# Two-block transformer on one core: retention heads turned inside the output product, a router with its weights stationary, the last expert by halves

## The reference

```python
logits = x @ w_router                     # 1024 x 8
top_val, top_idx = top_k(logits, 2); wts = softmax(top_val)
for e in range(8):                        # w_gate, w_up: 1024 x 3584, w_down: 3584 x 1024
    out = out + gates[..., e:e+1] * ((silu(x @ w_gate[e]) * (x @ w_up[e])) @ w_down[e])
x = layer_norm(ALPHA * x + out)
```

## Time and profile before

| | |
|---|---|
| runs | 1864.13 us median of 3 (1861.27 to 1864.32) |
| profiled execution, its own time | 1865.61 us |
| span of its trace, first to last instruction | 1863.8 us |
| TensorE busy | 1744.8 us (94%) |
| VectorE busy | 1416.8 us (76%) |
| ScalarE busy | 1028.3 us (55%) |
| GpSimd busy | 47.8 us (3%) |
| moved by DMA | 531.20 MB |
| mean granted TensorE clock | 0.970 of full |

### The profile page before, as it was taken

One profiled execution on the slowest core, in us unless ns is written; L12 is line 12 of the kernel. 1 busy time (PEld: TensorE's weight loads), 2 busy tenths in 40 slices (PEclk: granted clock), 3 DMA queues, 4 the chain that ended last, 5 costly groups with the idle time before them and its releaser, 6 DMA issues.

```text
span 1863.8 us, 23299 instructions
## 1 busy us (share of the span) xinstructions
PE 1744.8 (94%) x9360; PEld 1487.5 (80%) x9360; DVE 1416.8 (76%) x1241; ACT 1028.3 (55%) x828; POOL 47.8 (3%) x42
## 2 busy tenths in 40 slices
PE   2999899999889999997999999999999999999995
PEld 2988678878679997996888878878878888788784
DVE  7786856475965554775888988879879899798895
ACT  2343244553233333334777767768677777777672
POOL 0000002000000000001000000000000000000200
PEclk9999899999989999997999999999999999999997
DMA  9688354514727573554999999999999999999992
GB/s 366 213 334 298 129 207 152 181 57 154 230 99 270 182 270 136 204 204 147 363 365 382 386 352 389 376 377 375 367 367 364 372 376 377 373 387 370 366 386 96
DMA packets 217771, 531.20 MB, mean 285 GB/s; under 512 B 7600, under 2 KB 14016, under 8 KB 217408
## 3 DMA queue, kind: packets, MB, share of 16 engines
q1 hardware_dynamic: 210624, 514.52, 75.6%
q10 hardware_dynamic: 5712, 10.41, 1.5%
q0 software_dynamic: 1328, 4.73, 0.7%
HBM read 521.94 MB, written 16.09 MB: 289 GB/s over the span
## 4 chain that ended last, share of the span: by engine, by line
PE 70%; DVE 4%; DMA 2%; ACT 2%; issue 2%; POOL 0%; SPq 0%; POOLq 0%; DVEq 0%; ACTq 0%
PE psum L785 22%; PE psum L787 21%; PE psum L786 21%; DMA ring<-in_moe_w_gate 2%; DVE units L1607 2%; PE psum L1151 1%; PE psum L1052 1%; ACT units L1489 1%; PE psum L1005 0%; DVE R L1954 0%; PE psum L1089 0%; PE psum L1116 0%; PE psum L1124 0%; POOL root_out L1556 0%; PE psum L1023 0%
## 5 line engine op out<-in xcount | busy, mean ns | idle before, releaser
L1607 DVE TENSOR_TENSOR units<-ring,units 128x2048 fp32r<-128x2048 f32 x451 | 1010.9, 2278 | 258.9 <-ACT units L1258 151.8
L1489 ACT CAST units<-ring 128x2048 fp32r<-128x2048 f32 x332 | 624.4, 1912 | 239.5 <-PE psum L787 70.9
L785 PE MATMUL psum<-units,xr 128*128 128x512 f32 x1120 | 445.5, 398 | 14.2 <-DVE units L1607 7.1
L787 PE MATMUL psum<-units,xr 128*128 128x512 f32 x1120 | 439.5, 392 | 0.0
L786 PE MATMUL psum<-units,xr 128*128 128x512 f32 x1120 | 438.8, 392 | 0.0
L1258 ACT CAST units<-ring 128x2048 fp32r<-128x2048 f32 (+1 forms) x119 | 218.5, 1880 | 233.8 <-PE psum L787 186.4
L785 PE MATMUL psum<-units,H 128*128 128x512 f32 x696 | 274.5, 394 | 2.1 <-DVE H L1607 2.1
L787 PE MATMUL psum<-units,H 128*128 128x512 f32 x696 | 272.5, 391 | 0.0
L786 PE MATMUL psum<-units,H 128*128 128x512 f32 x696 | 272.4, 391 | 0.0
L785 PEld LDWEIGHTS psum<-units,xr 128*128 128x128 f32 x1120 | 212.2, 189 | 61.9 <-issue 7.8
L785 PE MATMUL psum<-xr,units 128*128 128x256 f32 x864 | 248.4, 287 | 7.3 <-DVE xr L1607 3.8
(11 more groups left out here) (260 smaller groups left out, 1007.2 us busy)
## 6 DMA issues: line engine op xcount, KB each, us to landing
ring<-in_moe_w_gate SPq DMA_DIRECT2D x56, 2048.0 KB, 9.7
ring<-in_moe_w_up SPq DMA_DIRECT2D x56, 2048.0 KB, 9.7
ring<-in_moe_w_down SPq DMA_DIRECT2D x56, 2048.0 KB, 9.6
ring<-in_mod_w SPq DMA_DIRECT2D x12, 2048.0 KB, 10.0
ring<-in_ret_w_in SPq DMA_DIRECT2D x11, 2048.0 KB, 9.6
ring<-in_fox_w_in SPq DMA_DIRECT2D x8, 2048.0 KB, 8.8
ring<-in_sc_w_in SPq DMA_DIRECT2D x6, 2048.0 KB, 8.2
ring<-in_ffn_w_gate SPq DMA_DIRECT2D x5, 2048.0 KB, 9.9
```

What stands on the lines that cost most here:

```text
L785: mm(dst, left[0], right[0], start=first, stop=False)
L787: return mm(dst, left[1], right[0], start=False, stop=last)
L1489: nc.scalar.copy(*expert_unit_parts(q, j, half, 0)).then_inc(unit_high, 1)
L1607: return v.tensor_tensor(dst, src, high.bitcast(F32), ALU.subtract)
```

## The change

Three places, in the order of the program.

**Retention.** `ret_read(2)` moves ahead of `token_chunk("ret_g", 3)`. The head's rows are first made without the root, `(o - mean) * silu(g)` in one VectorE pass, and ScalarE multiplies by the root (`ret_scale`). Head 0 is turned before `ret_read(3)`, heads 1 and 2 after it, and head 3 inside the output product after its first four blocks. The two `mod_w` loads of the second layer's gate, their sums and `mod_sum(1, GATE)` move from the output product and the fox queries to the fox values and gates.

**Router.** The router's 8 columns are stationary, the tokens move; the result (8 x 256) is copied and turned back by two transposes. Of VectorE's work after the choice only the slots stay ahead of the gather; the gates, the places, `e_acc` and the overflow flag come behind it. The first gather is split in two halves. VectorE reads the flag `over` before the experts.

**Last expert.** In the last four blocks of `down` the left half of the columns is finished first, put back and added while the right half is computed. The last layer norm stands at the end of the last expert, ahead of the branch, with both roots asked for at once; after the branch VectorE asks for two roots that nothing uses, since GpSimd's list of roots is fixed and now has those of the second sweep too.

```diff
-               CHUNK_AT["ret_out", 1]: [(1, GATE, 0)], CHUNK_AT["ret_out", 2]: [(1, GATE, 1)]}
+               CHUNK_AT["fox_g", 0]: [(1, GATE, 0)], CHUNK_AT["fox_g", 1]: [(1, GATE, 1)]}
...
-    g += [("ret_o", i, "D") for i in range(4)]
+    g += [("ret_o", i, "D") for i in range(6)]
     g += [("ret_g", i, "A") for i in range(6, 8)]
-    g += [("ret_o", i, "D") for i in range(4, 8)]
-    g += [("ret_uT", i, "S") for i in range(8)]
+    g += [("ret_uT", i, "S") for i in range(2)] + [("ret_o", i, "D") for i in range(6, 8)]
+    g += [("ret_uT", i, "S") for i in range(2, 8)]
...
             ret_read(0)
             ret_read(1)
+            ret_read(2)
             token_chunk("ret_g", 3)
...
+            ret_turn(0)
+            ret_read(3)
+            for h in range(1, RH - 1):
+                ret_turn(h)
+            out_product("ret_out", ruT, RV // P, lambda g: wait_emptied("ret_uT", g), lambda: ret_turn(RH - 1))
...
+            for k in range(KB):
+                if k % 2 == 0:
+                    wait_emptied("x5T", k // 2)
+                last = mm(b[0:NE, 0:T], w_router[:, k, :], x5T[:, k, :], start=(k == 0), stop=(k == KB - 1))
...
             for tt in range(NT):
-                for k in range(KB):
-                    last = mm(b[:, tt * NE:(tt + 1) * NE], x5T[:, k, tt * P:(tt + 1) * P], w_router[:, k, :],
-                              start=(k == 0), stop=(k == KB - 1))
+                last = nc.tensor.transpose(b[:, tt * NE:(tt + 1) * NE], scoresT[:, tt * P:(tt + 1) * P], ident[0:NE, 0:NE])
...
+                    halves = by_matmul(e, more, number) and k >= EB - ROWS
+                    for c in range(1 if halves else 2):
+                        last = down(k, c, w)
...
+                for k, w in late.items():
+                    if k == EB - ROWS // 2:
+                        pe.wait_ge(down_low, matmul_returns(e, number) + 1)
+                        scatter(0)
+                    last = down(k, 1, w)
...
+            def ret_scale(h):
+                act.wait_ge(root_ready, ROOTS.index(f"ret{h}") + 1)
+                wait_emptied("ret_o", 2 * h + 1)
+                for tt in range(NT):
+                    u = rg[:, tt, h * RHV:(h + 1) * RHV]
+                    nc.scalar.activation(u, u, ACT.Identity, scale=root_out[:, ROOTS.index(f"ret{h}") % 2, tt:tt + 1]
+                                         ).then_inc(ret_u_ready, 1)
...
-            high_in("ret_uT", ruT[0], 8)
+            high_in("ret_uT", ruT[0], 6)
+            highs_until(CHUNK_AT["ret_g", 3] + 2)
+            ret_scale(RH - 1)
+            high_in("ret_uT", ruT[0], 8, 6)
...
+            for h in range(RH - 1):
+                ret_head(h)
+            low_in("ret_uT", ruT, 2)
+            ret_head(RH - 1)
+            low_in("ret_uT", ruT, 6, 2)
+            lows_until(CHUNK_AT["ret_out", 1])
+            low_in("ret_uT", ruT, 8, 6)
+            lows_until(CHUNK_AT["ret_out", 3] + 1)
...
             select(0, 0)
+            low_half(CHUNK_AT["sc_out", 1] + 2, 1)
+            dve.wait_ge(first_high, 1)
+            low(e_x[0][1][:, 0:4, :], ...).then_inc(first_low, 1)
+            dve.wait_ge(gather_high, 1)
+            low(e_x[0][1][:, 4:8, :], ...).then_inc(gather_emptied, 1)
+            gates()
             places()
-            gathered(0, 0)
-            sweeps(dve, expert, start_second)
-            layer_norm("out", 4, e_acc, out_g, out_b)
+            for q in range(NT):
+                first_sums(q)
+            dve.wait_ge(up_emptied, 2)
+            overflow()
+            dve.wait_ge(sums_begun, NT)
+            sweeps(dve, expert, start_second, dve.value_load(over[0:1, 0:1], min_val=0, max_val=1))
+            for tt in range(NT):
+                ask_root(f"out1_{tt}", meanvar[:, tt, 1:2], 1.0, LN_EPS)
```

The end of the last expert on VectorE (`add_half(c)` waits for `scatter(c)` and adds 512 columns of each tile to `e_acc`):

```diff
+                    for c in range(2):
+                        dve.wait_ge(down_high, 2 * n + c + 1)
+                        low(e_y[1][:, cs], psum[:, c, :], e_y[0][:, cs]).then_inc(down_low if c == 0 else down_emptied, 1)
+                        if c == 0:
+                            add_half(0)
...
+                                    last = v.bn_stats(stats[:, tt, 0, :], e_acc[:, tt, 0:512])
...
+                add_half(1)
...
+                for tt in range(NT):
+                    ask_root(f"out{number}_{tt}", meanvar[:, tt, 1:2], 1.0, LN_EPS)
+                for tt in range(NT):
+                    v.scalar_tensor_tensor(x[:, tt, :], e_acc[:, tt, :], meanvar[:, tt, 0:1], out_g, ALU.subtract, ALU.mult)
+                for tt in range(NT):
+                    r = root(f"out{number}_{tt}")
+                    v.scalar_tensor_tensor(x[:, tt, :], x[:, tt, :], r[:, 0:1], out_b, ALU.mult, ALU.add)
```

More of the change, by code:

```diff
@@ L669, in sweeps @@
                 sweep(1)
+                if after is not None:
+                    after()
         block = ctx.enter_context(nc.Block())
@@ L853, in out_product @@
                 for k in range(blocks - tail):
+                    if k == ROWS and between is not None:
+                        between()
                     if k % 2 == 0:
@@ L948, in _, with ret_turn @@
             ret_read(1)
+            ret_read(2)
             token_chunk("ret_g", 3)
-            ret_read(2)
-            ret_read(3)
-            for h in range(RH):
+            def ret_turn(h):
                 pe.wait_ge(ret_u_ready, 2 * (h + 1))
@@ L1133, in wide_product @@
                 for half in range(2):
+                    if first and half == 1:
+                        pe.wait_ge(gather_emptied, 1)
                     w = expert_unit(e, q, j, half, lambda a: as_cols(a, 4))
@@ L1167, in expert, with down, scatter @@
                     pe.wait_ge(gather_emptied, e + 2)
+                def down(k, c, w):
+                    return product(psum[:, c, :], [a[:, k, :] for a in e_h],
+                                   [a[:, k % 2, c * 512:(c + 1) * 512] for a in w], k == 0, k == EB - 1)
+                def scatter(c):
+                    for tt in range(NT):
+                        for part in range(2):
+                            last = mm(psum[:, 2 * tt + c, :], e_selT[:, tt * P:(tt + 1) * P],
+                                      e_y[part][:, c * 512:(c + 1) * 512], start=(part == 0), stop=(part == 1))
+                    last.then_inc(scatter_filled, 1)
+                late = {}
                 for k in range(EB):
@@ L1194, in expert @@
                 pe.wait_ge(down_emptied, e + 2)
-                for tt in range(NT):
-                    for c in range(2):
-                        for part in range(2):
-                            last = mm(psum[:, 2 * tt + c, :], e_selT[:, tt * P:(tt + 1) * P],
-                                      e_y[part][:, c * 512:(c + 1) * 512], start=(part == 0), stop=(part == 1))
-                last.then_inc(scatter_filled, 1)
+                scatter(1)
             def start_second():
@@ L1302, in shifted_high, with high_in @@
                     last.then_inc(bank_high, 1)
-            def high_in(name, dst, n=4):
-                for g in range(n):
+            def high_in(name, dst, n=4, first=0):
+                for g in range(first, n):
                     nc.scalar.copy(dst[:, 2 * g:2 * g + 2, :], pairs(bank(name, g))).then_inc(bank_high, 1)
@@ L1609, in _, with low_half @@
             split = [0]
+            def low_half(m, half):
+                dve.wait_ge(unit_high, 2 * m + half + 1)
+                src, dst = unit_parts(m, half)
+                low(dst[1], src, dst[0]).then_inc(unit_ready, 1)
             def lows_until(n):
@@ L1621, in lows_until, with low_in @@
                 split[0] = max(split[0], n + 1)
-            def low_in(name, dst, n=4):
-                for g in range(n):
+            def low_in(name, dst, n=4, first=0):
+                for g in range(first, n):
                     dve.wait_ge(bank_high, high_count(BANK_AT[name, g]))
@@ L1804, in _, with ret_head @@
             ret_decay(3)
-            for h in range(RH):
+            def ret_head(h):
                 b = [bank("ret_o", 2 * h + tt) for tt in range(NT)]
@@ L2172, in places, with first_sums, overflow @@
+            def first_sums(q):
+                v.tensor_scalar(e_acc[:, q, :], x[:, q, :], ALPHA, None, ALU.mult).then_inc(sums_begun, 1)
+            def overflow():
+                for q in range(2):
+                    step(v.tensor_reduce(big[:, q:q + 1], counts[:, :], AX.X, ALU.max))
+                    v.tensor_scalar(over[:, :], big[:, q:q + 1], float(P), None, ALU.is_gt).then_inc(turn_emptied, 1)
+                dve.wait_ge(turn_emptied, 2)
             def places():
```

196 lines of the change are left out of this document (115 added, 81 removed).

## The result

The changed kernel took 1850.5 us (median of 4 runs, 1849.7 to 1854.9) beside 1864.2 for the kernel before (1861.3 to 1866.2); ratio 0.9934, 95% interval 0.9916 to 0.9952, so 9 to 16 us less. The profiled execution: 1850.9 us, span 1848.7 against 1863.8. The forecast was 1851.6, range 1845 to 1858.

The account below looks back on a forecast made before the run. TensorE works nearly the whole span, so only its idle and low-clock places can win. Retention 5.4, router 0.8 and end 6.3 sum to 12.5: median 1864.13 becomes 1851.6 us, range 1845 to 1858.

Parts of the forecast that it names:

- the 0.6 us from a shorter low clock: Retention, output product: of the 2.1 us that the low clock cost, 0.6 would be saved.
- each costs 0.85: 6.8 us, no less: Router product: 8 matmuls of 256 columns at the low clock cost 0.85 each, 6.8 us, against 7.00 before.
- 2 us more: Router product: extra gain if the clock rose halfway; no row showed that.
- 8.8 from it: Router, behind the gather: 8.8 us from GpSimd's first write to SP's load of chunk 4.
- some 8: Router: chunk 4 of the first expert's weights lands some 8 us after its load is issued.
- The main claim: Router to fifth chunk: chunk 4 is issued 6.4 us later, so 6.4 us of head start become 1.5.
- Head start kept: Rival, experts: the loads refill the lead within the first expert; 1846.4 us; chance 13%.
- loads bound: Rival, experts: the stage ends by the first load and the router part loses 3; 1855.4 us; chance 17%.
- the signs named for being wrong: No wait at chunk 4; expert stage over 5 us longer than 8 experts take now; SP's output DMA last.
- After it come the two unused requests, and GpSimd's two powers of 1.54: End, behind VectorE's branch: 3.0 jump, 0.2 requests and 3.1 powers follow 1851.2, ending at 1857.5; gain 6.3.
- GpSimd as the last engine: End, sign of being right: GpSimd ends last, with VectorE's 3 us jump before it.
- the output's DMA last: End, sign of being wrong: SP's output DMA ends last; forgetting the branch would put the end at 1855.5.

Follow-up runs that it names:

- the run with the sums put back: Changed kernel with the second layer's gate sums put back beside the output product, behind VectorE's low parts of the turned groups: 1862.0 us, ratio 0.9999.
- two runs of one edit: SyncE's load of the next expert's rows two chunk loads later: on the changed kernel 1841.9 us, ratio 0.9892; on the kernel before 1863.2, ratio 1.0004.
- the late read: Changed kernel with VectorE's read of the overflow flag put back behind its last pass: 1851.8 us, ratio 0.9944.

## Why the prediction was right, and where not

The number was right, 1851.6 for 1850.5; so were the places. The terms, with means over the traces that share a stretch:

**Retention.** Start of the product: predicted 206.35 from 212.19; measured 206.55, and 206.36 as the mean of nine traces with the part (the run with the sums put back left out), against a mean of 211.7 in four without. TensorE idles 3.1 ahead of it (predicted 2.8), VectorE's last head takes one pass of 1.40. The step that failed is the 0.6 us from a shorter low clock. The low clock ends 3.1 us into the product in the first trace, but after 3.0 to 6.1 us in the nine (mean 4.1) and 3.4 to 4.7 in the four (mean 4.1). From the product's start to the first transposes behind the residual the nine take 49.7 us on average, 48.7 without the turn of 1.0, and the four 48.7: nothing won. The gain there is 4.3, at the low end of 4.0 to 7.0. The 5.35 of the first pair, and the 6.7 by the router, lie above what the means give: over nine traces with the part and four without, the transposes ahead of the router come 4.0 us earlier. The size stays open all the same: that point lies anywhere from 837.6 to 843.8 in the nine traces, and the times of the part alone say 7.1 and 6.0 us, with 5.4 inside both intervals and 4.0 inside the second only. The sums cost nothing that the times can show, as said, and the earlier trace rows had the room for them. What I didn't see is what a less lucky place would have cost.

**Router.** The step "each costs 0.85: 6.8 us, no less" failed: the clock rose inside the product, 4.29 us, which I had priced at "2 us more" and given no row. The rule of the Trainium skill that weight loads go by columns ("TensorE: Matmul & The Clock Gate", section on LDWEIGHTS) would have given 4 us less; what was won is 2.5, and the windows put it down to the clock. The first expert matmul came 9.2 us earlier against the router's transposes (27.75 to 18.5), where I had 6.4. VectorE's chain behind the gather was right to 0.1: second place 5.3 us behind the gather's end (predicted 5.45), first write 1.03 later. But the four writes and the row load took 11.5 us to the issue of chunk 4 and not 8.8, since GpSimd's third and fourth write took 3.06 and 1.90 instead of 0.95 each: I had taken "8.8 from it" from the earlier trace rows, where VectorE idles beside the writes (a wait of 4.17 us up to 871.03); now it works beside them. So chunk 4 was issued 17.6 us behind the gather, not 15.2, and it landed 9.7 us later, not "some 8" (8.4 before), with two more loads issued within 1.3 us behind it. That makes the wait 8.63 and not 5.1. At the start of chunk 4, counted from the router's transposes, 1.0 us of the head start was left (50.5 against 51.5), predicted 1.5: nearly right, because a larger head start met a longer wait.

The main claim, that the head start dies in SyncE's queue, held and is shown by two runs of one edit. From the first expert matmul to the last four blocks TensorE took 959 to 961 us in five traces without the router part, 967 to 971.5 in six with it, and 959 to 960.3 in the three where the row load stands further back in the queue. Head start 9.2, lost 7 to 11: near zero by the profiles; by the times of the part alone 1.9 us won (from 5.0 won to 1.1 lost); predicted 0.8 won. "Head start kept" fell, and so did "loads bound": with DMA at 1.0 of its share all through the stage, a better order in one queue still gave 8.6. Of the signs named for being wrong, one came true here: the stage is 9 us longer from the first expert matmul on, over the 5 allowed. It stands for the larger head start and wait, not for a slower stage, as the waits behind 900 us show.

**End.** The last pass ends at 1845.07; with the 6.7 us by which all before it is earlier, that is 1851.8, predicted 1852.4. The step that failed is "After it come the two unused requests, and GpSimd's two powers of 1.54", with the 3.0 of the jump ahead of them on the path. The jump takes about 3 us here too, but from 1843.1, beside the last pass:

```profile
1843.79 1.28 DVE x L2373
1845.07 1.01 issue
1846.32 0.55 POOL root_out L1629
```

(the chain that ended last, changed kernel: start, us, step). Of the jump 1.0 us is left in front of VectorE's last requests, and the two powers take 1.06. At the very end two things meet, GpSimd's last entry and SyncE's wait for the output:

```profile
L316 POOLq DRAIN  x1: 1942/1942/1942, 1846.3 to 1846.3; - x1
SPq L316 <- DMA out<-x: 2.9, 1, 2.9
```

(changed kernel: duration in ns and start of the entry; total us, times and longest of the wait, which begins when the last store has been issued, at 1845.44). Both end at 1848.3, within 0.1 us of each other in both traces of this kernel, and the span ends at 1848.7. So what is left of the jump and the powers just fits beside the output's DMA. "GpSimd as the last engine", and the output's DMA last as a sign of being wrong, come out as a tie. With the late read GpSimd's entry ends at 1849.45, 0.8 us behind the landing. Over traces: from the start of the last four blocks, five old ends take 28.8 to 30.5 (mean 29.5), eight new ones with the early read 22.1 to 23.0 (mean 22.4). **7.1 won by the profiles, predicted 6.3**, inside its 5.0 to 8.3, and 5.6 (3.4 to 8.0) by the times of the part alone; the 8.4 of the pair had 1.5 from a last product at the low clock in the trace before (3.65 for the 2.11 of two other traces).

**Sum.** 4.0 + 0 + 7.1 = 11 by the traces, and 6.5 + 1.9 + 5.6 = 14 by the times of the parts; the times of the whole say 12.3 (9 to 16). The prediction's 12.5 lies between, from terms and steps each off by 1 to 3 us of both signs. It was the right mechanism, and some luck in the size.

## What to carry to other kernels

A head start is worth only what the next queue lets through: before moving steps behind an early start, list what each of them gates, and take loads that need nothing of them out from behind. Work that is moved "at no cost" must stand ahead of its engine's next long wait, not behind it; the same two sums cost nothing or 9 to 11 us. And split a change by its parts in several traces, for a stretch that no edit touched differed by 2 to 6 us between them.

## What the runs showed of the hardware

- The same product of the router ran its first part at 0.50 and the rest at 1.00 with 8 columns as weights and 256 streamed, and all of its 6.9 us at 0.50 with 128 as weights and 8 streamed, though TensorE was busy in all of every window (2.00 of 2.00) in both.
- GpSimd's four indirect writes took 1.08, 0.98, 0.95 and 0.95 us in the five traces without the router part, and 1.42, 0.98, 3.06 and 1.90 in the changed kernel. There VectorE's float32 passes with both inputs in SBUF run beside the third and fourth:

```profile
865.72 4.49 DVE L1680 TENSOR_TENSOR units<-ring,units 128x2048 fp32r<-128x2048 f32 x2 [1.41 <-issue]
867.93 2.28 DVE L1680 TENSOR_TENSOR units<-ring,units 128x2048 fp32r<-128x2048 f32 x1
```

  (changed kernel; the second row is the second of the two passes.) The passes end at 868.01 and 870.21, the writes at 868.83 and 871.04. In all nine traces with the router part the third and fourth write end 0.82 to 0.83 us behind the end of the pass that was running when they began: 18 of 18, whether they took 1.89 or 3.06. The first write, beside passes with one input over `x` (from 862.55), lost 0.34. A pass whose first input is in PSUM ran beside a whole write without a loss (the retention part alone, repeated):

```profile
864.31 1.23 DVE L1631 TENSOR_TENSOR xr<-psum,xr 128x1024 fp32r<-128x1024 f32 x1 [4.05 <-ACT xr L1518]
864.43 0.95 POOL L1589 DMA_INDIRECT x_rows<-x,place  x1 [0.30 <-issue]
```

  and a pass with two SBUF inputs that began 0.05 us behind a write's start left it at 0.98 (two traces). So the write waits for the end of such a pass. Likewise two powers took 2.77 us beside VectorE's passes and 1.06 when it had ended them. The Trainium skill ("SBUF — State Buffer", "SBUF: two separate sides") says that VectorE and GpSimd share a pair of ports which one of them holds for a whole instruction, and that a VectorE instruction with two SBUF inputs takes it only against a GpSimd instruction that reads SBUF. The rows agree, since the write reads the tile `place`; that the ports are the reason is argued and not shown.
- The same kernel waited 3.1 us more for a block written to memory and read back in one execution than in the next.
